# Sums of the scans' decays brought by transfers in a two-layer hybrid encoder on one core

## The reference

```
X = xs * dt;  a_cs = cumsum(dt * a)                    # within chunks of 128 positions
seg = a_cs[:, l] - a_cs[:, s];  decay = exp(where(s <= l, seg, -inf))
cb = C_l . B_s
y_diag = (cb * decay) @ X                              # within the chunk
states = B @ (X * exp(a_cs[-1] - a_cs))                # 4 chunks, carried along
y_off = (C @ s_in) * exp(a_cs)                         # from the chunks before
return y_diag + y_off
...
y = y_fwd + y_bwd + d_skip * xs                        # the same scan from both ends
y = rmsnorm(y * silu(z))
```

## Time and profile before

| | us |
|---|---|
| median of 3 runs | 1684.62 |
| the profiled execution's own time | 1684.64 |
| its span, first to last instruction | 1682.9 |
| PE busy (x8004) | 1659.0 |
| DVE busy (x1387) | 1001.9 |
| POOL busy (x339) | 687.4 |
| ACT busy (x932) | 679.8 |

### The profile page before, as it was taken

How to read it: one execution, slowest core, us unless ns; L and a number is a source line. 1 busy time by engine, 2 the same in 40 slices (tenths; PEclk the granted TensorE clock), 3 DMA queues, 4 the chain that set the end, 5 groups by cost and what they waited for, 6 DMA issues and landing times.

```text
span 1682.9 us, 20420 instructions
## 1 busy us (share of the span) xinstructions
PE 1659.0 (99%) x8004; PEld 1316.8 (78%) x8004; DVE 1001.9 (60%) x1387; ACT 679.8 (40%) x932; POOL 687.4 (41%) x339
## 2 busy tenths in 40 slices
PE   7999999999999999999999999999999999999999
PEld 5777787878778888888877777788777788888887
...
DMA packets 43231, 147.34 MB, mean 88 GB/s; under 512 B 5152, under 2 KB 5920, under 8 KB 43136
## 3 DMA queue, kind: packets, MB, share of 16 engines
...
q0 software_dynamic: 384, 0.75, 0.4%
...
## 4 chain that ended last, share of the span: by engine, by line
PE 89%; DVE 6%; issue 2%; ACT 1%; POOL 1%; DMA 0%; SPq 0%; DVEq 0%
PE banks L1080 27%; PE banks L1082 26%; PE banks L1081 26%; PE banks L1172 2%; PE banks L1151 2%; PE banks L1160 2%; PE banks L1255 1%; DVE sb_w_lo L747 1%; PE banks L1268 1%; PE banks L1227 1%; PE banks L1131 1%; DVE sb_e L822 1%; PE banks L1241 1%; PE banks L1211 0%; DVE sb_squares L735 0%
## 5 line engine op out<-in xcount | busy, mean ns | idle before, releaser
L360 POOL TENSOR_TENSOR sb_w_lo<-sb_w_raw,sb_w_hi 128x1024 fp32r<-128x1024 f32 x202 | 490.4, 2428 | 633.1 <-ACT sb_w_hi L453 633.1
L1080 PE MATMUL banks<-sb_h_hi,sb_w_hi 128*128 128x512 f32 x1360 | 558.2, 410 | 16.1 <-POOL sb_w_lo L360 10.7
L453 ACT ACTIVATE sb_w_hi<-sb_w_raw 128x1024 fp32r<-128x1024 f32 x258 | 272.6, 1057 | 671.4 <-PE banks L1082 665.1
L1082 PE MATMUL banks<-sb_h_hi,sb_w_lo 128*128 128x512 f32 x1360 | 537.3, 395 | 0.0
L1081 PE MATMUL banks<-sb_h_lo,sb_w_hi 128*128 128x512 f32 x1360 | 537.1, 395 | 0.0
L1080 PEld LDWEIGHTS banks<-sb_h_hi,sb_w_hi 128*128 128x128 f32 x1360 | 256.5, 189 | 99.5 <-issue 36.9
L1081 PEld LDWEIGHTS banks<-sb_h_lo,sb_w_hi 128*128 128x128 f32 x1360 | 256.9, 189 | 61.8 <-issue 6.9
L1082 PEld LDWEIGHTS banks<-sb_h_hi,sb_w_lo 128*128 128x128 f32 x1360 | 256.5, 189 | 60.1
L1045 DVE TENSOR_TENSOR banks<-banks,sb_rstd 128x512 f32<-128x512 f32 x88 | 61.5, 699 | 144.0 <-PE banks L1082 135.7
L1080 PE MATMUL banks<-sb_ff_hi,sb_w_hi 128*128 128x512 f32 x352 | 138.9, 395 | 0.0
L1082 PE MATMUL banks<-sb_ff_hi,sb_w_lo 128*128 128x512 f32 x352 | 138.9, 395 | 0.0
...
## 6 DMA issues: line engine op xcount, KB each, us to landing
sb_w_raw<-w_in SPq DMA_DIRECT2D x88, 512.0 KB, 3.4
sb_w_raw<-w_up SPq DMA_DIRECT2D x88, 512.0 KB, 3.3
sb_w_raw<-w_out SPq DMA_DIRECT2D x32, 512.0 KB, 3.4
sb_w_raw<-w_down SPq DMA_DIRECT2D x32, 512.0 KB, 3.3
sb_bias_t<-bias_rows SPq DMA_DIRECT2D x16, 448.0 KB, 6.0
sb_w_raw<-w_down SPq DMA_DIRECT2D x16, 384.0 KB, 3.0
sb_x_stream<-x_t SPq DMA_DIRECT2D x4, 512.0 KB, 6.7
...
```

The lines of the kernel that those rows point to most:

```text
L360: g.tensor_tensor(WLO[:, n % 2, :], W[:, n % 2, :], WHI[:, n % 2, :].bitcast(F32), ALU.subtract).then_inc(w_lo.handle, 1)
L453: sc.activation(WHI[:, n % 2, :], W[:, n % 2, :], ACT.Copy).then_inc(w_hi.handle, 1)
L1080: mm(out, whi, hhi, start=start, stop=False)
L1082: return mm(out, wlo, hhi, start=False, stop=stop)
```

## The change

The cumulated sums and their exponentials, 64 rows of 512 each, are written to two small tensors in DRAM (`store_rows`), and SP loads each head's two rows from there to all 128 partitions, straight into the head's buffer (`head_rows`, one transfer of 128x2x512); the exponentials of a pair of heads come the same way (`pair_exps`, two transfers of 128x384). The products of `row_sums`, the split of the sums and the selector go away. Banks 2 and 3, now free, hold the masked products `CB`. The difference with its cap is 8 operations of 128x128 a head, each with one column of sums as its operand. GpSimd adds the directions of all heads, so `within` has 8 instructions for 12. There are four head buffers.

The second group starts at slot 13, pairs are finished at G + 4, G + 6, ..., and the differences of a group's first three heads are made at G + 1 to G + 3, their exponentials with them, while their masked products follow one slot later.

```diff
-GROUP_AT = (2, 14)
-ROWS_AT = {GROUP_AT[h // 8] + 3 + h % 8: h for h in range(SSD_HEADS)}
-PAIR_AT = {GROUP_AT[t // 4] + 5 + 2 * (t % 4): t for t in range(SSD_HEADS // 2)}
+GROUP_AT = (2, 13)
+SEG_AT = {GROUP_AT[h // 8] + h % 8 + (1 if h % 8 < 3 else 2): h for h in range(SSD_HEADS)}
+WEIGH_AT = {GROUP_AT[h // 8] + 2 + h % 8: h for h in range(SSD_HEADS)}
+PAIR_AT = {GROUP_AT[t // 4] + 4 + 2 * (t % 4): t for t in range(SSD_HEADS // 2)}
...
-    HEAD_E = (E[:, 0, :, :], E[:, 1, :, :], SQ[:, :, :])
+    HEAD_E = (E[:, 0, :, :], E[:, 1, :, :], rm["e_third"][:, :, :], SQ[:, :, :])
...
+    CB = BANK[:, 2:4, :]
+    sum_rows = nc.dram_tensor("sum_rows", [2, 2 * DIR, SEQ], F32).ap()
...
+        def store_rows():
+            sp.wait_ge(*cs_row.at(1))
+            sp.dma_start(sum_rows[0, :, :], T[0:2 * DIR, 0, :]).then_inc(rows_stored.handle, 16)
+            sp.wait_ge(*cs_exp.at(1))
+            sp.dma_start(sum_rows[1, :, :], ER[0:2 * DIR, :]).then_inc(rows_stored.handle, 16)
+        def head_rows(h):
+            grp, n = h // 8, h % 8
+            if h == 0:
+                sp.wait_ge(*rows_stored.at(32))
+                sp.wait_ge(*at_pv.at(UNITS))
+            if n % 4 == 3:
+                sp.wait_ge(*st_mm.at(6 * grp + 6))
+            if h >= 4:
+                sp.wait_ge(*y_mm.at(2 * ((h - 4) // 2) + 2))
+            rows = bass.AP(sum_rows.tensor, h * SEQ, [[0, P], [DIR * SEQ, 2], [1, SEQ]])
+            sp.dma_start(head_e(h), rows).then_inc(rows_landed[h % 4].handle, 16)
+        def pair_exps(t):
+            if t >= 2:
+                sp.wait_ge(*y_read.at(t - 1))
+            for d in range(2):
+                rows = bass.AP(sum_rows.tensor, (2 * DIR + DIR * d + 2 * t) * SEQ + (P, 0)[d], [[SEQ, 2], [0, 64], [1, SEQ - P]])
+                sp.dma_start(EA[:, t % 2, d, :], rows).then_inc(ea_landed[t % 2].handle, 16)
...
+                slot = pos - POS["sc", 0]
+                if slot == 4:
+                    store_rows()
+                if slot - 2 in SEG_AT:
+                    head_rows(SEG_AT[slot - 2])
+                if slot - 1 in PAIR_AT:
+                    pair_exps(PAIR_AT[slot - 1])
...
-                if s in ROWS_AT and ROWS_AT[s] % 2 == 0:
-                    add_directions(ROWS_AT[s])
+                if s in WEIGH_AT:
+                    add_directions(WEIGH_AT[s])
...
-                if s in (20, 22, 24):
-                    gate(s // 2 - 6)
-                if s == 25:
+                if s in (20, 21, 22):
+                    gate(s - 16)
+                if s == 24:
                     gate(7)
...
-                    sc.activation(EA[half, (h // 2) % 2, :, :].rearrange("p d l -> p (d l)"),
-                                  BANK[half, 2:4, :].rearrange("p b s -> p (b s)")[:, P:P + 768], ACT.Exp).then_inc(ea_done.handle, 1)
...
-            v.tensor_tensor(head_e(h).rearrange("p d (c l) -> p d c l", l=P),
-                            BANK[:, 2:4, :].rearrange("p d (c l) -> p d c l", l=P), columns, ALU.subtract).then_inc(seg_read.handle, 1)
-            dve.wait_ge(*seg_read.at(h + 1))
-            v.tensor_scalar(head_e(h), head_e(h), 80.0, None, ALU.min).then_inc(seg_done.handle, 1)
+            dve.wait_ge(*rows_landed[h % 4].at(16 * (h // 4 + 1)))
+            for d in range(2):
+                for c in range(QT):
+                    at = slice(P * c, P * c + P)
+                    ins = v.tensor_scalar(head_e(h)[:, d, at], head_e(h)[:, d, at], AS[:, c, column(d, h):column(d, h) + 1], 80.0,
+                                          ALU.subtract, ALU.min)
+            ins.then_inc(seg_done.handle, 1)
...
-        def row_sums(h):
...
-            for d in range(2):
-                ins = mm(bank(2 + d), SEL[:, column(d, h):column(d, h) + 1].to_broadcast([P, P]), CS[:, :], start=True, stop=True)
...
-            pe.wait_ge(*gs_done.at(t + 1))
-            pe.wait_ge(*g_done.at(2 * t + 2))
+            pe.wait_ge(*gs_done.at(2 * t + 2))
...
-                for h, d in ((2 * t, 0), (2 * t + 1, 0), (2 * t + 1, 1)):
+                for h in (2 * t, 2 * t + 1):
                     half = 64 * (h % 2)
                     ins = mm(BANK[half:half + 64, 6 + t % 2, P * c:P * c + P], XT[:, c, 64 * (h % 8):64 * (h % 8) + 64],
-                             head_e(h)[:, d, P * c:P * c + P], start=d == 0, stop=d == h % 2)
-                    if c == QT - 1 and d == h % 2:
+                             head_e(h)[:, 0, P * c:P * c + P], start=True, stop=True)
```

More of the change, by code:

```diff
@@ L159, in build_trunk @@
     con = {n: CON[:, i, :] for i, n in enumerate(CONSTS)}
-    SEL = sb("selectors", [P, 64], F32R)
     PAR = sb("params", [P, DEPTH, PA_N])
@@ L208, in build_trunk @@
     QHI, QLO, KHI, KLO = (rm[n] for n in ("q_high", "q_low", "k_high", "k_low"))
-    XT, SIN, BT, CS, EA, CB, E = (rm[n] for n in ("x_tok", "s_in", "b_tok", "cs", "exp_cs", "cb", "e"))
-    HEAD_E = (E[:, 0, :, :], E[:, 1, :, :], SQ[:, :, :])
+    XT, SIN, BT, ER, EA, E = (rm[n] for n in ("x_tok", "s_in", "b_tok", "exp_rows", "exp_cs", "e"))
+    HEAD_E = (E[:, 0, :, :], E[:, 1, :, :], rm["e_third"][:, :, :], SQ[:, :, :])
     SCC, CX, SCA, SCP, Z = (rm[n] for n in ("sc_c", "sc_cx", "sc_acc", "sc_prod", "z"))
@@ L233, in build_trunk @@
     x_stored = sem("x_stored")
-    sel_done, eps_done = sem("sel_done"), sem("eps_done")
+    eps_done = sem("eps_done")
+    rows_stored = sem("rows_stored", 32)
+    rows_landed = [sem(f"rows_landed{i}", 64) for i in range(4)]
+    ea_landed = [sem("ea_landed0", 128), sem("ea_landed1", 128)]
     bias_mm, bias_row = sem("bias_mm"), sem("bias_row")
@@ L258, in build_trunk @@
         sem(n, 1) for n in ("dt_tr", "dt_x", "dt_e", "dt_w", "dt_ln", "a_exp", "dt_done", "lndt_done", "da_done"))
-    cs_mm, cs_row, cs_hi, cs_lo, cs_tr, cs_col, dec_mm, dec_exp, ws_done = (
-        sem(n, 1) for n in ("cs_mm", "cs_row", "cs_hi_done", "cs_lo_done", "cs_tr", "cs_col", "dec_mm", "dec_exp", "ws_done"))
+    cs_mm, cs_row, cs_exp, cs_tr, cs_col, dec_mm, dec_exp, ws_done = (
+        sem(n, 1) for n in ("cs_mm", "cs_row", "cs_exp", "cs_tr", "cs_col", "dec_mm", "dec_exp", "ws_done"))
     tok_tr, tok_copied = sem("tok_tr", 10), sem("tok_copied", 10)
     cb_mm, cb_done, xs_done, st_mm, sin_done = sem("cb_mm", 2), sem("cb_done", 4), sem("xs_done", 12), sem("st_mm", 12), sem("sin_done", 12)
-    ab_mm, seg_read, seg_done, e_done, ea_done, g_done, y_mm = (
-        sem(n, SSD_HEADS) for n in ("ab_mm", "seg_read", "seg_done", "e_done", "ea_done", "g_done", "y_mm"))
-    gs_done = sem("gs_done", SSD_HEADS // 2)
+    seg_done, e_done, g_done, gs_done, y_mm = (
+        sem(n, SSD_HEADS) for n in ("seg_done", "e_done", "g_done", "gs_done", "y_mm"))
     yo_mm, y_read, t_read, z_copied, y_comb = (sem(n, 8) for n in ("yo_mm", "y_read", "t_read", "z_copied", "y_comb"))
@@ L270, in head_e @@
     def head_e(h):
-        return HEAD_E[h % 8 % 3]
+        return HEAD_E[h % 4]
     def par(col, n=1):
@@ L599, in _ @@
             for s, (kind, i) in enumerate(SLOTS):
-                if s in ROWS_AT:
-                    h = ROWS_AT[s]
-                    half = slice(64 * (h % 2), 64 * (h % 2) + 64)
-                    act.wait_ge(*seg_read.at(h + 1))
-                    if h >= 4:
-                        act.wait_ge(*y_read.at(h // 2 - 1))
-                    sc.activation(EA[half, (h // 2) % 2, :, :].rearrange("p d l -> p (d l)"),
-                                  BANK[half, 2:4, :].rearrange("p b s -> p (b s)")[:, P:P + 768], ACT.Exp).then_inc(ea_done.handle, 1)
+                if s in SEG_AT:
+                    h = SEG_AT[s]
                     act.wait_ge(*seg_done.at(h + 1))
@@ L620, in _ @@
                     sc.activation(T[0:64, 0, :], BANK[0:64, 2, :], ACT.Copy).then_inc(cs_row.handle, 1)
-                    sc.activation(CS[0:64, :], BANK[0:64, 2, :], ACT.Copy).then_inc(cs_hi.handle, 1)
+                    sc.activation(ER[0:64, :], BANK[0:64, 2, :], ACT.Exp).then_inc(cs_exp.handle, 1)
                     act.wait_ge(*dec_mm.at(1))
@@ L1103, in block_of, with tile @@
                 ins.then_inc(w_used.handle, 1)
-        def tile(kind, i, width=P, head=None):
+        def tile(kind, i, width=P):
             for k in range(KT):
-                if k == KT // 2 and head is not None:
-                    row_sums(head)
                 block_of(kind, i, k, width)
@@ L1270, in from_states, with output_first @@
             ins.then_inc(yo_mm.handle, 1)
-        def output_first(m, head):
+        def output_first(m):
             s, b = weights("o1", m), tile_bank("o1", m)
             for k in range(KT):
-                if k == KT // 2 and head is not None:
-                    row_sums(head)
                 at = slice(P * k, P * k + P)
@@ L1345, in _ @@
                 if kind == "o1":
-                    output_first(i, ROWS_AT.get(s))
+                    output_first(i)
                 else:
-                    tile(kind, i, head=ROWS_AT.get(s))
+                    tile(kind, i)
```

45 lines of the change are left out of this document (10 added, 35 removed).

## The result

| | before | after |
|---|---|---|
| median, us | 1684.46 (4 runs) | 1699.50 (1697.48 to 1700.10, 4 runs) |
| span of the profiled execution | 1682.9 | 1698.3 |
| PE busy (x records) | 1659.0 (x8004) | 1644.5 (x7812) |
| PE's waits in the scan stage | 4.4 | 35.5 |

The ratio is 1.0086, with a 95% interval of 1.0073 to 1.0099. The forecast was 1679.6, faster by 5. Both layers lose about the same: the last product of the sums of squares in the first layer comes 7 us later than before, and the second layer adds 8. Within the first layer, the tile of slot 14, which began at 323.60, begins at 326.94; but 2.1 us of this are the transposes of the second group, which now stand ahead of this tile and stood ahead of the next. So the first group loses 1.2 us, where a gain of 1.7 was forecast, and the rest of the layer, in the main the second group, 5.7, where a gain of 0.8 was forecast.

The account below looks back on a forecast made before the run. PE was taken as the bound (89% of the chain), with DVE nearly as full in the scan stages. Of 16.1 us a layer 1.7 + 0.8 = 2.5 arrive, 5.0 in two layers: 1684.6 - 5.0 = 1679.6 us, range 1665 to 1700.

Parts of the forecast that it names:

- PE's savings: Scan stages: row sums save 15.0 us, pair products (1.89 to 1.02 us) 13.9; together 28.9, none under cover.
- The small operations: DVE's eight 128x128 operations a head: 0.20 us each, 1.6 a head, saving DVE 0.23 a head.
- Transfers: SP's loads of head rows and exponentials: 0 cost, with 1.5 us at a tight slot as the other end.
- rival A: Exponentials' loads use 2 of 16 DMA engines at 19.5 GB/s each: +12 us on the forecast, 1692; chance 0.24.
- The pairs' waits: PE waits for the odd head's GpSimd sum: 1.8 us at pair 0, 0.2 at pair 3, 2.7 at pair 7.
- The wait at slot 22: Second group: PE comes earlier and DVE's `w_lo` later, so PE waits 3 us at slot 22.
- Collisions: GpSimd's sums hold up DVE's small operations: 1 us at 6 of 8 heads, +6 us in the first group.
- What DVE keeps: First group: DVE is nearly full, so the group gains 1.7 of PE's 8.1 us; bounds 0 and 6.
- The second group's earlier start: Scans end two slots sooner, but the last sum of squares hangs on ACT's and GpSimd's chain: 0.
- Rival B: DVE and GpSimd eat all, by small operations at 0.27 us or a collision at every head: 1684; chance 0.18.
- rival C: No collisions, GpSimd's sum starts ahead of `w_lo`; first group gains 6, second 2: 1668; chance 0.14.
- Rival D: All engines reading the same 4 KB is slow, a slot's loads take 12 us against 7: over 1740; chance 0.10.

Follow-up runs that it names:

- fills: 8 extra PE products, values unread, ahead of the waits at pairs 0, 3, 7: four transfers 1690.1 to 1683.3 us; changed kernel 1699.5 to 1696.3.
- four transfers: Changed kernel with a pair's exponentials loaded in four transfers of 64 partitions instead of two of 128, same bytes: 1690.1 us against 1699.5.

## Why the prediction was wrong

The forecast of 1679.6 and the result lie 19.9 us apart. By the runs: 9.4 us are the two-engine loads (1699.5 to 1690.1), 6.8 the granted clock behind PE's waits at pairs (1690.1 to 1683.3), and 3.7 remain. The split holds for this order of edits: part of the 9.4 is clock too (49 slow products against 28), and in the changed kernel the same fills gave 3.2.

- **PE's savings** were right: 1.02 forecast and 1.03 measured for a pair, 192 records, 28.9 us. The busy time fell by 14.5 and not by 29, since products at the lower clock take longer.
- **The small operations** came out at the 0.20 us forecast, but not from the rows named: these (0.40 us for 512 elements, 0.61 for 1024) give 0.21 for 512 elements more, so 0.19 fixed and 0.24 for a small one. The 0.27 in its place stands in no row, and no run here takes a small operation apart.
- **Transfers** is the step that failed first: "0, with 1.5 us at a tight slot as the other end". The mechanism stood in the text as rival A and had a rule behind it, but the forecast was taken without it. Its price was 12 us, and the runs gave 9.4. The sign given for it came: DVE waits for transfers, 20.5 us in all, up to 4.3 at once. But A's working does not hold: it had the two engines fall behind at 19.5 GB/s each, and at the measured 25 its own terms give an estimated 13.1 us of transfers for two slots (393 kB over 50 GB/s, and 131 kB over 25), less than the 13.9 that they last. What was late is single loads that stood behind the exponentials in the queue. That I gave A 0.24 rested on DVE's pace "leaves it little to delay": but DVE is what the late rows delay.
- **The clock had no term in the sum.** It counted a wait of 2.7 us as 2.7 us. The trace before could not show it, since the longest wait of PE there was 0.88 us in this stage, and its clock was full throughout. A range that takes in new waits of 2 to 4 us had to hold it.
- **The pairs' waits** had the right cause, the release and 2.21 us of the sum, and pair 7's came out longest, but they were too small: 0.2, 1.8 and 2.7 us forecast at pairs 3, 0 and 7, 2.72, 2.52 and 3.63 measured; over a layer 6.1 forecast for sums and 10.7 measured. Pair 3's was off by most: of the 2.6 us by which its masked product used to be ready before PE, nothing was left. Late rows were not the cause, since with four transfers the wait is 2.74; what took this slack stays open.
- **The wait at slot 22** was forecast as 3 us for a `w_lo`. What came was 4.24 us at slot 21 (383.62), for DVE's z, behind 3.36 us of late rows at 375.30, and none at slot 22. With four transfers it is 1.19 us at slot 21, and at slot 22 the `w_lo` has 1.62: the cause was there, at half the size.
- **Collisions** were in the sum at 6 us for the first group. Four small operations of it took over 1 us, 3.4 us in all more than the others' 0.28, and 16 further GpSimd operations that nobody waited for cost 0.3 us, at most 2.4. The step was too dear; what made the group late were waits for data.
- **"What DVE keeps"** was right in kind: with every wait for a sum gone, PE's saving of 13.9 us arrives at 4.1.
- The second group's earlier start had 0 in the sum; put back by a slot, the kernel was 3.8 us slower, with a wait behind the SiLU. Rival B's 0.27 for a small operation did not come, and rival C's "no collisions" did not either. Rival D is excluded as to size: head rows land in 5.0 us at the least, slower than the 3.4 of a weight, but leaving out 24 of the 32 loads gave 1.0 us.

Open: 3.7 us of the gap to the forecast, 2 us in the account of PE, and pair 3's slack. That waits, not something beside them, bring the clock down rests on the fills; by how long a wait or how much work was not tried.
